# A relative-bias table computed as one strip a head, stored in 128 copies and read back askew

## The reference

```python
def rel_bucket(dist):                       # 32 buckets over the distance
    ...
    return jnp.where(dist < max_exact, dist, jnp.minimum(log_b, REL_BUCKETS - 1))
...
dist = jnp.maximum(t_pos[None, :, None] - idx, 0)        # query position minus key position
bias = jnp.moveaxis(rel_bias[rel_bucket(dist)], -1, 2)   # rel_bias: 32 buckets x 8 heads
logits = einsum('bqhc,bqkc->bqhk', ql, c_sel) * ATT_SCALE + bias
```

## Time and profile before

| what | value |
|---|---|
| median of 3 executions | 3278.92 us (3277.60 to 3282.61) |
| the profiled execution | 3278.26 us |
| its span in the trace | 3276.3 us |
| granted TensorE clock, mean | 0.96 |
| TensorE busy | 2994.2 us, 91% of the span |
| VectorE, ScalarE, GpSimd busy | 1416.2, 931.3 and 1281.4 us |

### The profile page before, as it was taken

The page is one execution under the profiler, slowest core; times in us unless marked ns, Lnnn a source line. Parts: engine busy times, 40 slices in busy tenths (PEclk is TensorE's granted clock), DMA queues, the critical chain, the costliest instruction groups (busy, mean ns, idle before and its releaser), DMA issues.

```text
span 3276.3 us, 38179 instructions
## 1 busy us (share of the span) xinstructions
PE 2994.2 (91%) x12758; PEld 2254.8 (69%) x12762; DVE 1416.2 (43%) x2317; ACT 931.3 (28%) x1609; POOL 1281.4 (39%) x623
## 2 busy tenths in 40 slices
PE   6999989887799899997899899998779999899998
PEld 2688866664377588885576678886547777688886
DVE  7211232885323511135446555533734453455425
ACT  3211012333311311103345333302235551233202
POOL 0455443221044455544422255544431112455544
PEclk9999998988899899998899999999889999999999
DMA  4232321101022132331222122332211111232322
GB/s 158 77 95 91 94 80 60 57 28 49 13 77 96 58 94 92 92 95 65 80 87 78 58 77 90 94 95 74 80 52 33 39 35 63 77 96 90 93 87 97
DMA packets 78601, 249.31 MB, mean 76 GB/s; under 512 B 9073, under 2 KB 15729, under 8 KB 78385
## 3 DMA queue, kind: packets, MB, share of 16 engines
q1 hardware_dynamic: 64800, 229.74, 22.5%
q10 hardware_dynamic: 13712, 18.44, 1.7%
HBM read 238.57 MB, written 9.44 MB: 76 GB/s over the span
## 4 chain that ended last, share of the span: by engine, by line
PE 82%; DVE 8%; ACT 4%; issue 2%; POOL 1%; DMA 1%; ACTq 0%; DVEq 0%; POOLq 0%; SPq 0%
PE ps L297 23%; PE ps L299 23%; PE ps L298 23%; DVE tmp L493 2%; PE ps L2414 1%; PE ps L2455 1%; PE ps L2433 1%; PE ps L2434 1%; PE ps L1293 1%; PE ps L1116 1%; PE ps L1949 1%; PE ps L452 1%; POOL xl L481 1%; PE ps L1934 1%; DVE xl L481 1%
## 5 line engine op out<-in xcount | busy, mean ns | idle before, releaser
L291 POOL TENSOR_TENSOR w_lo<-raw,w_hi 128x1024 fp32r<-128x1024 f32 (+1 forms) x438 | 1037.9, 2370 | 1551.0 <-DVE w_hi L284 1551.0
L297 PE MATMUL ps<-xh,w_hi 128*128 128x512 f32 x2184 | 886.3, 406 | 54.5 <-DVE xl L481 30.3
L284 DVE CAST w_hi<-raw 128x1024 fp32r<-128x1024 f32 (+1 forms) x438 | 331.0, 756 | 1252.7 <-PE ps L299 1200.9
L298 PE MATMUL ps<-xl,w_hi 128*128 128x512 f32 x2184 | 868.4, 398 | 0.0
L299 PE MATMUL ps<-xh,w_lo 128*128 128x512 f32 x2184 | 867.9, 397 | 0.0
L297 PEld LDWEIGHTS ps<-xh,w_hi 128*128 128x128 f32 x2184 | 412.6, 189 | 190.6 <-issue 48.1
L298 PEld LDWEIGHTS ps<-xl,w_hi 128*128 128x128 f32 x2184 | 413.8, 189 | 101.9 <-issue 5.7
L299 PEld LDWEIGHTS ps<-xh,w_lo 128*128 128x128 f32 x2184 | 413.0, 189 | 101.6
L299 PE MATMUL ps<-ah,w_lo 128*128 128x512 f32 x704 | 278.1, 395 | 0.0
L297 PE MATMUL ps<-ah,w_hi 128*128 128x512 f32 x704 | 278.1, 395 | 0.0
L298 PE MATMUL ps<-al,w_hi 128*128 128x512 f32 x704 | 278.1, 395 | 0.0
(11 more groups left out here) (367 smaller groups left out, 3724.1 us busy)
## 6 DMA issues: line engine op xcount, KB each, us to landing
raw<-in_ffn_up SPq DMA_DIRECT2D x90, 512.0 KB, 3.5
raw<-in_conv_up SPq DMA_DIRECT2D x88, 512.0 KB, 3.5
raw<-in_ffn_down SPq DMA_DIRECT2D x32, 512.0 KB, 3.5
raw<-in_conv_down SPq DMA_DIRECT2D x32, 512.0 KB, 3.5
raw<-in_merge SPq DMA_DIRECT2D x24, 512.0 KB, 3.6
raw<-in_ple_gate SPq DMA_DIRECT2D x24, 512.0 KB, 4.4
raw<-in_diff SPq DMA_DIRECT2D x24, 512.0 KB, 3.5
raw<-in_mla SPq DMA_DIRECT2D x20, 512.0 KB, 3.5
```

Source lines behind the costliest of these rows:

```text
L284: dve.tensor_copy(self.w_hi[s][:, 0:n], self.raw[r][:, 0:n]).then_inc(self.sem["slot_hi"], 1)
L291: pool.tensor_tensor(self.w_lo[s][:, 0:n], self.raw[r][:, 0:n], self.w_hi[s][:, 0:n].bitcast(F32), ALU.subtract).then_inc(self.sem["slot_s ...
L297: pe.matmul(out, wh, xh, start=start, stop=False)
L298: pe.matmul(out, wh, xl, start=False, stop=False)
```

## The change

Table 0 is no longer made by `BiasTable` but by a new stage `BiasStrip`. It works out the bias of 640 consecutive distances (511 down to -128) for each head, once: 32 buckets on the partitions, 640 distances along the row, two matrix products with 8 output rows. The 8 x 640 result is then stored 128 times over in one DMA, so that in HBM each head has 128 copies of its row of 640, one after the other. The sparse attention reads 128 rows of 512 with a pitch of 639: each row then starts one element earlier in its copy than the last one did, which is the shift by one that the next query needs. The input loads shrink with it, and ScalarE waits for the store before it reads the strip back.

```diff
+STRIP = T + P                      # 640
...
-        strip = k.dram["strip"].rearrange("(q h) s -> h q s", h=HEADS)
+        strip = k.dram["strip"][:, P - 1:P - 1 + P * (STRIP - 1)].rearrange("h (q w) -> h q w", w=STRIP - 1)[:, :, 0:T]
+        act.wait_ge(k.dma["strip_stored"], k.dma_total["strip_stored"])
...
+class BiasStrip(Stage):
+    def load(self, act):
+        k = self.k
+        act.dma_start(k.sdisti[:], k.dram["dist"].to_broadcast([BUCKETS, STRIP])).then_inc(k.dma["bias_in0"], 16)
+        act.dma_start(k.stab[:].rearrange("p a h -> p (a h)"), k.dram["table0"]).then_inc(k.dma["bias_in0"], 16)
...
+    def tensor(self, pe):
+        k = self.k
+        pe.wait_ge(*self.on("strip_step", 1))
+        pe.wait_ge(*self.on("strip_step", 2))
+        pe.matmul(k.ps[0:HEADS, 2, 0:T], k.stab[:, 0, :], k.ssel[:, 0:T], start=True, stop=True)
+        pe.matmul(k.ps[0:HEADS, 3, 0:STRIP - T], k.stab[:, 0, :], k.ssel[:, T:STRIP], start=True, stop=True
+                  ).then_inc(k.sem["strip_mm"], 1)
+
+    def scalar(self, act):
+        k = self.k
+        act.wait_ge(*self.on("strip_mm"))
+        act.activation(k.sout[:, 0:T], k.ps[0:HEADS, 2, 0:T], ACT.Copy).then_inc(k.sem["strip_out"], 1)
+        act.activation(k.sout[:, T:STRIP], k.ps[0:HEADS, 3, 0:STRIP - T], ACT.Copy).then_inc(k.sem["strip_out"], 1)
+        act.wait_ge(*self.on("strip_out", 1))
+        act.dma_start(k.dram["strip"].rearrange("h (q w) -> h q w", w=STRIP),
+                      k.sout[:].unsqueeze(1).to_broadcast([HEADS, P, STRIP])).then_inc(k.dma["strip_stored"], 16)
+
+    def vector(self, dve):
+        k = self.k
+        dve.wait_ge(k.dma["bias_in0"], self.loads)
+        dve.tensor_copy(k.sdist[:], k.sdisti[:]).then_inc(k.sem["strip_step"], 1)
+        dve.tensor_tensor(k.stab[:, 0, :], k.stab[:, 0, :], k.stab[:, 1, :], ALU.subtract
+                          ).then_inc(k.sem["strip_step"], 1)
+        dve.wait_ge(*self.on("strip_step", 0))
+        dve.tensor_scalar(k.ssel[:], k.sdist[:], k.starts[0:BUCKETS, :], None, ALU.is_ge
+                          ).then_inc(k.sem["strip_step"], 1)
...
-    tables = [BiasTable(k, 0, "table0", "iota", "strip", [NB - 1], NB - 1, False),
-              BiasTable(k, 1, "table1", "pos", "bias", range(NB), 0, True)]
+    tables = [BiasStrip(k), BiasTable(k, 1, "table1", "pos", "bias", range(NB), 0, True)]
...
-    dram["strip"] = nc.dram_tensor("strip", (P * HEADS, T), F32).ap()
+    dram["strip"] = nc.dram_tensor("strip", (HEADS, P * STRIP), F32).ap()
```

More of the change, by code:

```diff
@@ L146 @@
  gate prod_a prod_b merged v_out rope_made
+ strip_step strip_mm strip_out
  bias_step bias_sel bias_mm bias_out rope_step rope_rot""".split()
-DMA_SEMS = "loaded x_here stored kidx_copied bias_in0 bias_in1 positions_in bias_stored0 bias_stored1 tile_in0 tile_in1".split()
+DMA_SEMS = "loaded x_here stored kidx_copied bias_in0 bias_in1 positions_in bias_stored0 bias_stored1 strip_stored tile_in0 tile_in1".split()
 class Kernel:
@@ L212, in __init__ @@
             (self.bpos, self.bposi, self.brow, self.browi, self.bsel, self.bout, self.btab, self.bdiag, self.lamv,
-             self.lams),
+             self.lams, self.sdist, self.sdisti, self.ssel, self.sout, self.stab),
         ) = overlay(
@@ L254, in __init__ @@
              ("bsel", [P, 8, T], F32), ("bout", [P, 2, T], F32), ("btab", [P, 2, 2, HEADS], F32),
-             ("bdiag", [P, 2, 32], F32), ("lamv", [P, 4, 64], F32), ("lams", [P, 8], F32)],
+             ("bdiag", [P, 2, 32], F32), ("lamv", [P, 4, 64], F32), ("lams", [P, 8], F32),
+             ("sdist", [BUCKETS, STRIP], F32), ("sdisti", [BUCKETS, STRIP], I32), ("ssel", [BUCKETS, STRIP], F32),
+             ("sout", [HEADS, STRIP], F32), ("stab", [BUCKETS, 2, HEADS], F32)],
         )
@@ L1582, in gpsimd, with __init__, plan, on @@
                                    ALU.subtract).then_inc(k.sem["x_lo"], 1)
+class BiasStrip(Stage):
+    def __init__(self, k):
+        self.loads = k.moved("bias_in0", 2)
+        super().__init__(k)
+        self.joined = True
+    def plan(self):
+        k = self.k
+        self.e = k.events(1, strip_step=range(3), strip_mm=[0], strip_out=[0, 1])
+        self.stored = k.moved("strip_stored")
+    def load(self, act):
+        k = self.k
+        act.dma_start(k.sdisti[:], k.dram["dist"].to_broadcast([BUCKETS, STRIP])).then_inc(k.dma["bias_in0"], 16)
+        act.dma_start(k.stab[:].rearrange("p a h -> p (a h)"), k.dram["table0"]).then_inc(k.dma["bias_in0"], 16)
+    def on(self, name, key=0):
+        return self.k.sem[name], self.e.at(name, key)
+    def tensor(self, pe):
[14 more added lines that the diff above has]
+    def vector(self, dve):
+        k = self.k
+        dve.wait_ge(k.dma["bias_in0"], self.loads)
[5 more added lines that the diff above has]
+                          ).then_inc(k.sem["strip_step"], 1)
 class BiasTable(Stage):
@@ L2969 @@
     arrays["level_masks"] = np.concatenate(masks, 1).astype(np.float32)
-    for n, (table, name, pos) in enumerate(((a["rel_bias"], "iota", np.arange(T, dtype=np.int32)),
-                                            (a["rel_bias_table_2"], "pos", a["positions_2"][0]))):
+    for n, (table, copies) in enumerate(((a["rel_bias"], 1), (a["rel_bias_table_2"], 4))):
         before = np.concatenate([np.zeros_like(table[:1]), table[:-1]])
-        arrays[f"table{n}"] = np.tile(np.concatenate([table, before], 1), (4, 1))
-        arrays[name] = pos.reshape(1, T)
-        arrays[name + "_rows"] = np.ascontiguousarray(pos.reshape(P, 4).T)
+        arrays[f"table{n}"] = np.tile(np.concatenate([table, before], 1), (copies, 1))
+    arrays["dist"] = np.arange(T - 1, T - 1 - STRIP, -1, dtype=np.int32).reshape(1, STRIP)
+    arrays["pos"] = a["positions_2"][0].reshape(1, T)
+    arrays["pos_rows"] = np.ascontiguousarray(a["positions_2"][0].reshape(P, 4).T)
     arrays["lam"] = np.concatenate([a[n][0] for n in ("a_lam_q1_2", "a_lam_k1_2", "a_lam_q2_2", "a_lam_k2_2")])[None]
```

## The result

The changed kernel takes 3312.28 us (median of 4 executions, 3310.91 to 3312.51) against 3278.71; the ratio is 1.0101, with a 95% interval of 1.0088 to 1.0113. It is slower by 33.6 us, where 29.3 were forecast (3308, range 3268 to 3318).

What follows compares the result with a forecast made beforehand. Table 1's stores were taken to bound the first 80 us; the strip's landing moves its third copy from 40.12 to 69.4, +29.3, giving 3278.26 + 29.3 = 3307.6, with the median 0.7 above, so 3308, range 3268 to 3318.

Steps and rivals of the forecast that it cites:

- What bounds the stretch: First 80 us: table 1 goes at its stores' pace with two `bout` buffers; moving its end, 80.05, moves the kernel's end.
- What is taken away: Table 0 replaced by the strip stage: table 1's first `bsel` at 18.5 in place of 36.24, 17.7 us earlier.
- The rate of the store: Strip's store from eight neighbouring partitions: two paths out of SBUF, 51.8 GB/s, 50.6 us; the forecast case has chance 0.62.
- the row of `kidx`: Evidence for the store's rate: 128 KB copied from 64 partitions took 2.2 us, against 1.7 for a store from 128.
- one (101 us, +79.7): Rival for the strip's store: one path for all eight partitions, 101 us, landing 119.5, kernel 3358; chance 0.05.
- the engines' limit (12.7 us): Rival for the strip's store: eight engines limit it, partitions do not; landing at 31.2, kernel about 3271; chance 0.13.
- The landing: Strip's store: issued at 17.2, plus 1.3 fixed and 50.6 transfer, lands at 69.1; table 1's third copy at 69.4.
- Queued transfers wait for one another: ScalarE's DMA queue: table 1's stores wait behind the strip, as `raw` loads behind `h` took 11.6 us to land.
- the later stores do not wait: Part of the nearly-hidden rival: table 1's stores pass the strip; 13 to 17.7 us faster, 3261 to 3266; chance 0.12.
- The issue that holds ScalarE: At the strip's store: issuing many descriptors might hold up ScalarE, delaying table 1's start and adding 3.9 us.
- Two small terms that cancel: At table 1's restart: two ready banks gain up to 0.5 us; TensorE's low clock after idling costs about as much.
- Costed at nothing: Askew strip reads hidden by some 4 us of cover, ScalarE's wait before them, later `h` and `raw` landings: no cost.

Runs made afterwards that it cites:

- the last run, above: 128-partition store issued after table 1's last store, with table 0's five input loads put back on ScalarE's queue, against that late kernel: 3261.55 us, 0.9949 of the first kernel.
- The runs with 128, 8 and 4 paths: Changed kernel with the strip stored from 128 partitions (3267.50 us), eight partitions four apart (3272.68) or eight sixteen apart (3286.02).
- a step of 4: Changed kernel with the eight heads' rows on partitions 0, 4, 8 .. 28 in place of 0 .. 7: 3272.68 us, 0.9982 of the first kernel.
- the late run: Changed kernel with the strip stored from 128 partitions, issued after table 1's last store and waited for in `BiasesStored`: 3261.67 us, 0.9954 of the first kernel.
- a step of 16: Changed kernel with the eight heads' rows on partitions 0, 16, 32 .. 112 in place of 0 .. 7: 3286.02 us, 1.0021 of the first kernel.

## Why the prediction was right

- **What bounds the stretch.** Right: table 1's stores set its pace, and the whole shift of its end (+32.9) is in the end result (+33.6 by medians).
- **What is taken away.** 17.7 us forecast, 15.3 measured (36.24 to 20.95). The constants landed 1.46 later: the four loads fewer, which were to save nothing, go with a later landing (the last run, above). TensorE needed 2.3 us for 1.8, and the strip's own issue held ScalarE for 1.35 us and not 0.34, with the Exp of `lams` behind it.
- **The rate of the store.** Right, and it was the choice that decided the sign. Two paths of 25.9 GB/s gave 50.6 us; its packets took 51.0. That partitions count, and not engines alone, was argued from the row of `kidx`. That it is two paths and not one (101 us, +79.7) no row decided: "need not all lie on the same one" is a guess that came true. The runs with 128, 8 and 4 paths show that it is the partitions' ways out of SBUF: the engines' limit (12.7 us) shows only with a step of 4, where the packets took 13.7. That rival was priced right, for a kernel that was not this one.
- **The landing.** 73.5 for 69.1: 1.5 from the later issue, 0.4 from the rate, 2.5 mostly because the first packet went only 3.6 us after the issue, at 22.27, while the first weight loads still ran. This and nothing else is the difference between +29.3 and +33.7 at the third copy.
- **Queued transfers wait for one another.** The step gave the right time for the wrong reason. The stores did wait, but on SyncE's queue the strip costs nearly the same (3307.09). The row of `raw` behind `h` can't tell a shared queue from shared engines, and I took it for the former; the packets on two queues show shared engines. The case "the later stores do not wait" was therefore much less likely than it looked, even for another queue.
- **The issue that holds ScalarE.** Named as a chance of 3.9 us; it happened, 15.60 and 4.00 us long, and cost nothing, because table 1 had already begun.
- **Two small terms that cancel.** At the restart they did no harm: the clock was low as forecast (products of 419 ns for 285), and still table 1 from its third copy on took 39.1 us for 39.9. But a second low stretch, in the norm, has no term in the sum: the norm took 2.9 us more. By the profiles 33.7 - 0.8 + 2.9 is 35.8, and the spans differ by 34.3; that so little is left of these terms beside the third copy's shift is luck.
- **Costed at nothing.** Right for the askew reads (2.7 us to land, and no wait for them in the trace) and for `h` and `raw`.

## What to carry to other kernels

Before a small tile is written out many times, ask from how many partitions it is read, and which: eight rows on neighbouring partitions left at 51 GB/s, the same eight four apart at 191, and sixteen copies made by the matrix product on 128 partitions at 341, beside other traffic, with the strip issued 0.2 us later (18.95 for 18.72). A slow transfer is not out of the way because it has another queue or a far deadline, for it holds its engines and all other traffic that needs them; make it short, then put it where it is covered (13.0 us to land in the late run). When work is removed from a start-up stretch, the first wait behind it (here a double buffer that waits for its stores) says whether the gain arrives.

## What was not expected of the hardware

- A 64 KB store on ScalarE's queue, issued while a narrow store was under way on SyncE's, took some 20 us in place of 1.5; weight loads of 512 KB took 19.7 in place of 3.5. In both, half of a transfer's packets went at once and the other half waited.
- The issue of a store is held when the narrow one is ahead of it: 15.60 us in the changed kernel, 7.07 with a step of 16, 2.43 with a step of 4, 0.38 with 128 partitions. On the other queue the second store is held for 4.09.
- A read of 128 rows of 2048 B at a pitch of 2556 B landed in 2.7 us, no slower than the aligned one (3.0).
